# Dilated attention by groups of four heads instead of pairs: order, buffers and banks

## The reference, cut to what matters

```python
y_ssd = ssd_mixer(xbc, dt_raw, z, dt_bias[i], a_log[i], d_skip[i], ssd_norm[i])
q = rms_norm_2(q.reshape(b, s, ATT_HEADS, ATT_HEAD_DIM), q_norm[i])
k = rms_norm_2(k.reshape(b, s, ATT_HEADS, ATT_HEAD_DIM), k_norm[i])
y_att = dilated_attention(q, k, v).reshape(b, s, ATT_WIDTH)
x = x + jnp.concatenate([y_ssd, y_att], axis=-1) @ w_out[i]
```

## Time and profile before

| | us |
|---|---|
| median of 3 runs (1887.22 to 1887.64) | 1887.54 |
| the profiled execution | 1887.55 |
| its span, first to last instruction | 1885.8 |
| TensorE matmuls busy | 1878.2 |
| TensorE weight loads busy | 1628.2 |
| VectorE busy | 1451.7 |
| ScalarE busy | 1170.4 |
| GpSimd busy | 397.5 |

### The profile page before, as it was taken

How to read it: one execution, slowest core, us unless ns; L and a number is a source line. 1 busy time by engine, 2 the same in 40 slices (tenths; PEclk the granted TensorE clock), 3 DMA queues, 4 the chain that set the end, 5 groups by cost and what they waited for, 6 DMA issues and landing times.

```text
span 1885.8 us, 29598 instructions
## 1 busy us (share of the span) xinstructions
PE 1878.2 (100%) x11164; PEld 1628.2 (86%) x11164; DVE 1451.7 (77%) x2607; ACT 1170.4 (62%) x2165; POOL 397.5 (21%) x456
## 2 busy tenths in 40 slices
PE   9999999999999999999999999999999999999999
PEld 8889988897898888888988788888888898878887
DVE  6877996677799769866787978757885687897874
ACT  6667785567678556545667565545554667756552
POOL 2210211011011005411022214402440102223430
PEclk9999999999999999999999999999999999999999
DMA  9344566543465656665554355555555544445553
GB/s 354 124 141 145 194 204 204 173 152 123 136 196 192 206 170 205 190 195 180 179 167 136 124 189 190 190 191 186 192 190 191 189 158 153 150 145 185 189 193 127
DMA packets 92333, 334.62 MB, mean 177 GB/s; under 512 B 10240, under 2 KB 10784, under 8 KB 91808
## 3 DMA queue, kind: packets, MB, share of 16 engines
q1 hardware_dynamic: 92192, 332.73, 53.6%
HBM read 331.61 MB, written 1.08 MB: 176 GB/s over the span
## 4 chain that ended last, share of the span: by engine, by line
PE 91%; DVE 6%; ACT 2%; issue 1%; DVEq 0%; ACTq 0%
PE PS L83 88%; PE PS L86 3%; DVE WL L98 2%; DVE TMP L98 1%; DVE TMP L108 1%; DVE TMP L105 1%; ACT TMP L95 1%; ACT WH L92 1%; DVE SM L114 1%; DVE M L108 0%; DVE SM L108 0%; ACT TMP L92 0%; ACT M L92 0%; ACT TMP L94 0%; DVE SM L105 0%
## 5 line engine op out<-in xcount | busy, mean ns | idle before, releaser
L98 DVE TENSOR_TENSOR WL<-RAW,WH 128x1024 fp32r<-128x1024 f32 (+1 forms) x610 | 760.1, 1251 | 281.5 <-ACT WH L92 277.8
L92 ACT ACTIVATE WH<-RAW 128x1024 fp32r<-128x1024 f32 (+1 forms) x610 | 640.1, 1053 | 310.0 <-PE PS L83 305.3
L83 PE MATMUL PS<-WH,GX 128*128 128x512 f32 (+1 forms) x1636 | 524.7, 392 | 0.0
L83 PE MATMUL PS<-HX,WH 128*128 128x512 f32 (+1 forms) x1920 | 523.5, 344 | 0.4
L83 PE MATMUL PS<-HX,WL 128*128 128x256 f32 x1488 | 413.9, 281 | 0.0
L83 PE MATMUL PS<-GX,WH 128*128 128x256 f32 (+1 forms) x1776 | 409.6, 330 | 0.4
L83 PEld LDWEIGHTS PS<-HX,WH 128*128 128x128 f32 x1920 | 331.1, 189 | 46.6 <-DVE TMP L108 0.8
L83 PEld LDWEIGHTS PS<-WH,GX 128*128 128x128 f32 x1636 | 306.2, 188 | 64.6 <-issue 3.7
L83 PEld LDWEIGHTS PS<-GX,WH 128*128 128x128 f32 x1776 | 298.0, 190 | 30.2 <-DVE TMP L108 0.8
L83 PE MATMUL PS<-WL,GX 128*128 128x512 f32 (+1 forms) x818 | 317.1, 388 | 0.0
L98 POOL TENSOR_TENSOR TMP<-TMP,RB 128x256 f32<-128x256 f32 x176 | 205.6, 1172 | 473.5 <-DVE TMP L98 235.1
(11 more groups left out here) (146 smaller groups left out, 1679.4 us busy)
## 6 DMA issues: line engine op xcount, KB each, us to landing
RAW<-wts SPq DMA_DIRECT2D x607, 512.0 KB, 4.3
CUM<-rows SPq DMA_DIRECT2D x8, 512.0 KB, 4.9
M<-bias SPq DMA_DIRECT2D x4, 320.0 KB, 11.7
M<-bias SPq DMA_DIRECT2D x1, 1280.0 KB, 8.8
X<-x SPq DMA_DIRECT2D x2, 512.0 KB, 10.9
M<-mem SPq DMA_DIRECT2D x1, 1024.0 KB, 13.0
M<-memt SPq DMA_DIRECT2D x1, 1024.0 KB, 11.4
CST<-cst SPq DMA_DIRECT2D x1, 794.0 KB, 12.6
```

The source lines that it names most:

```text
L83: return Issued(self.eng and self.eng.matmul(o, l, r, start=first, stop=last, skip_group_check=share))
L92: return Issued(self.eng.activation(o, i, f, scale=scale))
L98: return Issued(self.eng and self.eng.tensor_tensor(o, a, b, op))
```

## The change

The dilated attention goes by groups of four heads (`by_fours`) on TensorE, ScalarE and VectorE; GpSimd's order stays. The scores of two pairs come together, four transposes follow with a beat behind each, then the sums of the two pairs back to back, into two halves of bank 6, which are read once both are there. In the first group the `yield` stands between the two pairs' scores. The third and fourth head of a group have their scores in banks 5 and 6 (first group) or 0 and 1 (later). All engines take their beats from one `DIL_RATES`: 15 fill steps instead of 14, and eight prepared ones in four beats of two, all in banks 0 and 1. All gate tiles go to banks 2 and 7, their product follows one tile later. The scores with the table get three buffers instead of two, the probabilities four instead of two, two of them in SQ, which holds the cumulative rows (hence a wait for `rows_out`).

```diff
-        def src_t(i):
+        def src_t(a, i):
+            if a[0] == "dil":
+                return TMP[:, i % 3 * 384:i % 3 * 384 + 384]
...
         def exp_t(a, i):
             if a[0] == "dil":
-                return TMP[:, 1024 + i % 4 * 384:1408 + i % 4 * 384]
+                return TMP[:, 1152 + i % 4 * 384:1536 + i % 4 * 384]
...
         def prob_t(a, i):
+            if a[0] == "dil":
+                if i % 4 < 2:
+                    return TMP[:, 2688 + i % 4 * 384:3072 + i % 4 * 384]
+                return SQ.rearrange("p k s -> p (k s)")[:, i % 2 * 384:i % 2 * 384 + 384]
...
-        DIL_RATES = [1, 1, 1] + [1, 1, 0] * 3 + [0, 1, 0] * 5
-
-        PREP_RATES = [0, 0, 0] + [0, 1, 0] + [1, 1, 0] + [0, 0, 0] + [1, 0, 0] * 5
-        DIL_PARTS = [0, 0, 0] + [2, 2, 1] + [1, 1, 0] * 2 + [0, 1, 0] * 5
+        DIL_RATES = [1, 1, 1, 0, 0] + [1, 1, 1, 1, 0] + [1, 0, 1, 1, 0] * 2 + [0, 1, 0, 1, 0]
+
+        PREP_RATES = [0, 0, 0, 0, 0] * 2 + [0, 2, 0, 0, 0] * 2 + [2, 0, 2, 0, 0]
...
-                        ps.append(take((a, "s", j), SCB[j % 2:j % 2 + 1]))
+                        banks = SCB
+                        if a[0] == "dil" and j % 4 >= 2:
+                            banks = (5, 6) if j < 4 else (0, 1)
+                        ps.append(take((a, "s", j), banks[j % 2:j % 2 + 1]))
...
                 def weigh(i):
-                    if two:
+                    if a[0] == "dil":
+                        o = i % 2 * 256
+                        if i % 2 == 0:
+                            take((a, "o", i), OB)
+                        else:
+                            BANK[a, "o", i] = BANK[a, "o", i - 1]
+                            holds[BANK[a, "o", i]] = (a, "o", i)
+                        os = [bank((a, "o", i))[64 * u:64 * u + 64, o:o + 256] for u in range(2)]
+                    elif two:
...
+                def by_fours():
+
+                    for k in range(n // 2 + 1):
+                        if k < n // 2:
+                            scores(2 * k)
+                            if k == 0:
+                                yield
+                            scores(2 * k + 1)
+                        for u in range(4):
+                            if k >= 1:
+                                turn_probs(4 * k - 4 + u)
+                            fill.beat(next(rate))
+                            prep.beat(PREP_RATES[5 * k + u])
+                        if k >= 1:
+                            weigh(2 * k - 2)
+                            weigh(2 * k - 1)
+                        fill.beat(next(rate))
+
+                if a[0] == "dil":
+                    yield from by_fours()
+                    return
...
-                        fm_tile(("z", L, m), whole, WT if m >= 2 else (0, 1))
+                        fm_tile(("z", L, m), whole, (2, 7))
...
-                        ps = take(("xd", L, b), (0, 1) if b < 3 else STB)
+                        ps = take(("xd", L, b), (0, 1))
...
-                        ps = take(("cb", L, g), STB)
+                        ps = take(("cb", L, g), (0, 1))
...
                 def probs(j):
-                    if j >= 2 and two:
+                    if a[0] == "dil":
+                        if j == 3:
+                            e.wait_ge(rows_out, a[1])
+                        if j >= 4:
+                            e.wait_ge(weighed, (a, j // 2 - 2))
+                    elif j >= 2 and two:
                         e.wait_ge(weighed, (a, j // 2 - 1))
...
                 def high(i):
-                    e.wait_ge(weighed, (a, i))
+                    e.wait_ge(weighed, (a, i | 1 if a[0] == "dil" else i))
...
+                def by_fours():
+
+                    for k in range(n // 2 + 1):
+                        for u in range(4):
+                            if k >= 1:
+                                probs(4 * k - 4 + u)
+                            if k < n // 2:
+                                exps(4 * k + u)
+                            if k == 0 and u == 1:
+                                yield
+                            fill.beat(next(rate))
+                        if k >= 1:
+                            high(2 * k - 2)
+                            high(2 * k - 1)
+                        fill.beat(next(rate))
+
+                if a[0] == "dil":
+                    yield from by_fours()
+                    return
...
-                    both = a[0] == "dil" and i >= 2 or not two and i == n
+                    both = not two and i == n
...
-                dilated = attention(("dil", L), dil_heads(L), [128, 256], fill, DIL_PARTS)
+                dilated = attention(("dil", L), dil_heads(L), [128, 256], fill, DIL_RATES)
...
-                        e.wait_ge(ahi, (a, d))
+                        e.wait_ge(ahi, (a, d | 1 if a[0] == "dil" else d))
...
-                        src = src_t(j)
-                        if j >= 2:
-                            e.wait_ge(exped, (a, j - 2))
+                        src = src_t(a, j)
+                        back = 3 if a[0] == "dil" else 2
+                        if j >= back:
+                            e.wait_ge(exped, (a, j - back))
...
+                def by_fours():
+
+                    for k in range(n // 2 + 1):
+                        if k < n // 2:
+                            maxima(4 * k)
+                            maxima(4 * k + 1)
+                        if k == 0:
+                            yield
+                        for u in range(4):
+                            if k < n // 2:
+                                if u < 2:
+                                    maxima(4 * k + 2 + u)
+                                inverse(4 * k + u)
+                            if u < 2 and k >= 2:
+                                low(2 * k - 4 + u)
+                            fill.beat(next(rate))
+                            prep.beat(PREP_RATES[5 * k + u])
+                        fill.beat(next(rate))
+                    low(n - 2)
+                    low(n - 1)
+
+                if a[0] == "dil":
+                    yield from by_fours()
+                    return
...
-                        if 2 <= m < 7:
-                            z_end(m - 2)
-                        if m >= 6:
+                        if m >= 1:
                             z_end(m - 1)
```

More of the change, by code:

```diff
@@ L501, in keys_of, with out_of @@
             return slice(o, o + widths[t])
+        def out_of(a, i):
+            o = i % 2 * 256 if a[0] == "dil" else 0
+            return bank((a, "o", i))[:, o:o + 256]
         def exps_of(widths, t):
@@ L802, in attention @@
                         fill.beat(next(rate))
-                        if prep is not None:
-                            prep.beat(PREP_RATES[3 * i + u])
                     if i >= 1 and two:
@@ L1246, in exps @@
                         e.wait_ge(small, (a, "max", j))
-                    src = src_t(j) if biased else bank((a, "s", j))
+                    src = src_t(a, j) if biased else bank((a, "s", j))
                     if a[0] == "na":
@@ L1272, in high @@
                 def high(i):
-                    e.wait_ge(weighed, (a, i))
+                    e.wait_ge(weighed, (a, i | 1 if a[0] == "dil" else i))
                     if two:
                         d = heads[2 * i]["dst"]
-                        o = bank((a, "o", i))[:, 0:256]
+                        o = out_of(a, i)
                         if a[0] in ("na", "gqa"):
@@ L1940, in low @@
                             continue
-                        e.tt(GL[:, d, :], bank(o)[:, 0:256], GH[:, d, :].bitcast(F32), ALU.subtract).then_inc(
-                            alo, (a, d), o)
+                        src = out_of(a, i) if two else bank(o)[:, 0:256]
+                        e.tt(GL[:, d, :], src, GH[:, d, :].bitcast(F32), ALU.subtract).then_inc(alo, (a, d), o)
                 def maxima(j):
@@ L2529, in block2 @@
                 fill = Steps(others())
-                dilated = attention(("dil", L), dil_heads(L), [128, 256], fill, DIL_PARTS, prep=Steps(prepared()))
+                dilated = attention(("dil", L), dil_heads(L), [128, 256], fill, DIL_RATES, prep=Steps(prepared()))
                 for i in range(KD):
```

## The result

| | before | after |
|---|---|---|
| median of the comparison, us | 1887.55 (1887.22 to 1887.64) | 1915.74 (1914.03 to 1916.83) |
| span of the profiled execution, us | 1885.8 | 1914.7 |
| mean granted clock of TensorE over the span | 1.000 | 0.994 |
| TensorE matmuls busy, us | 1878.2 | 1886.1 |

The ratio is 1.0149, 95% interval 1.0136 to 1.0161: slower by 28.2 us, where 16.3 was forecast and the range ended at 1913. The direction was right and the size was not. The rival in which the clock falls came true, and it too was priced too low.

A forecast was written before the change was run, and what follows sets the result against it. TensorE, busy nearly the whole span, was taken as the bound. Per layer, 9.75 us of waits A to E plus 1.5 in the state-space stretch, less 1.6 and 1.5 saved, gave 8.15; both layers 16.3, so 1904 us, range 1894 to 1913.

The forecast's parts named there:

- The rival in which the clock falls: TensorE's granted clock falls to half speed at wait A, losing 1.5 to 3.2 us each time; 1909 us, chance 0.22.
- A: Scores of pair 1, first group: TensorE waits 3.5 us for ScalarE's copy to free bank 6; low bound 2.6.
- C: First gate (z) tile, banks 2 and 7: waits 2.0 us for ScalarE to evict the second values.
- B: First two conv-output transposes, banks 0 and 1: wait 0.5 and 1.3 us for VectorE's multiply-adds on heads 10 and 11.
- D: Next group's conv-output transposes: wait 1.7 us for VectorE to finish head 15 in the same banks; bounds 1.0 and 2.0.
- E: Fifth gate (z) tile: waits 0.75 us for the third's product, behind a ScalarE weight-half copy; bounds 0.3 and 1.0.
- Merging: Merged score and sum blocks on TensorE: fewer entries, returns and block overheads save 1.6 us a layer; bounds 0 and 1.8.
- old stalls: TensorE stalls of the kernel before, hanging on single banks and short cover: all go, 1.5 us a layer; bounds 0 and 1.5.
- The state-space stretch: Behind the attention: TensorE has 2.97 us less work, VectorE only 1.5 less, so 1.5 lost a layer; bounds 0 and 2.
- Bank 6 was not free in time: Answers the rival that pair 1's bank is free in time, so A goes, 2 x 3.5 us: 1897, chance 0.11.
- The merging saves: Answers the rival that merging saves nothing and old stalls move on: 2 x (1.6 + 1.5) us more, 1910, chance 0.06.
- Faster: Rival: ScalarE and VectorE catch up within each group, so only savings count: 1881.3 us, chance 0.07.

The follow-up runs named there:

- a_early_copy: Changed kernel with ScalarE's last copy of transposed queries moved ahead of the first two exponentials of the dilated attention; 1905.82 us, ratio 1.0097.
- c_values_early: Changed kernel with ScalarE's eviction of the second values one beat earlier; 1906.23 us, ratio 1.0100.
- bd_prep_late: Changed kernel with the four transposes of conv outputs issued two steps later in their group of heads; 1908.99 us, ratio 1.0116.
- k_keep_all: k_keep_busy with four dummy products also ahead of the conv transposes of the third and fourth groups, filling B and D; 1907.33 us, ratio 1.0104.
- abcd_apart: abcd with the weighted sums of each first pair a step earlier, so no two sums stand back to back; 1894.77 us, ratio 1.0038.
- tuned_v5: tuned_v4 with VectorE's fourth-group gate-tile step ahead of the third maximum, and the fifth and sixth pairs' products ahead of the decays; 1888.52 us, ratio 1.0005.
- k_keep_busy: Changed kernel with dummy matmuls of constants filling two waits, eight products in A and five in C; 1908.59 us, ratio 1.0116.
- abcd: Changed kernel with the three repairs a_early_copy, c_values_early and bd_prep_late together; 1892.85 us, ratio 1.0028.
- tuned_v3: Changed kernel with early copy and eviction, fill reordered, second values' last parts and last gate tile moved up; 1893.15 us, ratio 1.0030.
- tuned_v4: tuned_v3 with the second values' parts and the last gate tile left where the changed kernel has them; 1889.11 us, ratio 1.0009.
- tuned_v7: tuned_v5 with VectorE's fourth-group gate-tile step one maximum earlier and only the fifth pair's product ahead of the decays; 1891.03 us, ratio 1.0019.

## Why the prediction missed

**The clock, the step that failed.** The prediction set "no stall that I found before is over 0.4" and "no row shows it fall between two matmuls" against the fall, gave it 0.22 and priced one fall a layer, 2.4. The rows said more than was taken from them: at the end of the program the clock is already down 1.8 us after TensorE's work stops, and A was forecast at 3.5. A kernel whose longest stall is 0.2 is no evidence on one of 3.5. The number was wrong as well, because C was not asked the same question: there were two falls a layer, which cost 4.0 and 5.2 us, so 2.0 and 2.6 a fall. The price of one fall was right and their count was not. That is 9.3 of the 12.6 us by which the span's 28.9 exceeds 16.3. The rule of the Trainium skill ("TensorE: Matmul & The Clock Gate", section "Why this matters for your kernels") against idle gaps between bursts of matmuls agrees with wait A, the longest, and was worth more than the chance it got. That falls also came behind waits of 2.0 and 1.9 us, shorter than A, is what these runs add to it.

**The new waits.** As idle time, forecast and measured: A 3.5 and 3.45; B 0.5 + 1.3 and 0.65 + 1.03; C 2.0 and 2.02; D 1.7 and 1.89; E 0.75 and 0.79. Together 9.75 and 9.83, each with the releaser named; a_early_copy, c_values_early and bd_prep_late remove A, C, and B with D; E was not tried alone. Small error: the forecast was from start to start, and a stop also breaks the flow. A cost 990.42 - 986.57 - 0.33 = 3.52, and read in the same way, from start to start, the six stops come to some 10.7, an estimate.

**Merging and old stalls.** The eighth gate tile starts at 1054.86 instead of 1043.26, 11.6 later. Less 4.0 of clock that is 7.6; in k_keep_all, without the clock, it starts at 1050.78, 7.5 later. And 10.7 - 7.6 = 3.1: the forecast's 1.6 + 1.5, as far as the estimate of 10.7 is right. abcd_apart shows 0.24 a pair of sums for its part; the old stalls weren't tried alone, so their 1.5 is only what is left of the sum.

**The state-space stretch.** From that gate tile to the third normalisation's transposes it took 38.76 before and 41.00 after: 2.2 lost against 1.5, just over the bound of 2. VectorE is at 38.95 of 41.14 us, 95% and not over 96%; the price was taken from its load, while in the trace TensorE waits 0.75 and 0.40 there for products that stand behind four decays in VectorE's order. In tuned_v5, with two of them ahead of the decays, the wait of 0.75 is one of 0.21 and that of 0.40 is gone, but the one for the normalisation grows to 0.70.

**In sum**, for the span: 16.3 forecast, 9.3 of clock, 2 x 0.7 behind, 2 x 0.9 of lost flow at the stops: 28.8 of 28.9; the last two terms are what was left over and partly estimated, so that the sum closes proves little for them. That the sum without the clock was 3 us short did not matter; that a rival was left at half its price did. Without the clock the kernel would be at 1907.3, inside the range.

**The other rivals.** Bank 6 was not free in time. The merging saves. "Faster" was to decide from the point where A to E come under 3 us a layer: tuned_v5 has 2.3 us of idle a layer in all (1.3 + 0.7 + 0.3) and is level, not faster, so that point was put too kindly: by the forecast's own prices it should have been faster, and where the difference goes wasn't tried.

## What to carry to other kernels

When a change makes TensorE wait for some two microseconds or more (here every wait of 2.0 and 3.4 us had a fall behind or around it in the profiled executions, and some shorter ones did), price the half clock at each such wait as part of the forecast and not as a rival, and fill the waits with dummy matmuls in one run to separate the two. A bank that is given to a new user is free when its old reader's engine gets to it in that engine's own order: write the order down for each reader, as for A to D, since it was right within 0.3 us. And when a wait is repaired, look at what the repair now stands in front of, and at whether another repair has already taken the same half clock away; three repairs worth 26 us alone gave 23 together.

## What the runs showed of the hardware

- The stretches at half clock came in two lengths only, 3.41 and 6.83 us, in both layers of the five kernels that have them.
- Which wait brought a fall was not a matter of that wait alone. D's 1.9 us had none behind it in the changed kernel and in c_values_early, and had one in a_early_copy and in the second layer of k_keep_busy; B's 0.65 and 1.03 had one in the first layer of k_keep_busy only. Single waits of 1.3 to 1.7 us in abcd, abcd_apart, tuned_v3, tuned_v4 and tuned_v7 had none. All this is of profiled executions: k_keep_busy varies from 1.000 to 0.996 in mean clock between executions, and three of tuned_v3's seven have 0.999. What decides between these was not settled.
- In the first layer the clock is full through all of wait A and falls 0.9 us after the work is back; in the second it falls at 1598.85, 0.9 us before the scores start at 1599.77. Either way most of the half clock falls on work. At half, a 512-wide matmul follows the last after 0.43 us instead of 0.23:

```profile
991.87 0.63 PE L83 MATMUL PS<-WL,GX 128*128 128x512 f32 x1
992.30 0.63 PE L83 MATMUL PS<-WH,GX 128*128 128x512 f32 x1
...
1599.77 0.59 PE L83 MATMUL PS<-M 64*128 64x128 f32 x2 [3.35 <-ACT M L92]
```
